# Weight splits of the latent-attention loop moved from VectorE to GpSimd

## The chip, the cores and the metric

One core of one Trainium2 chip. The metric is the device time of one execution in microseconds, median of several runs. Engines: PE is TensorE, DVE is VectorE, ACT is ScalarE, POOL is GpSimd, SP issues most of the DMAs.

## What is computed

Two blocks of two layers each on 512 tokens of width 1024, all in float32. The last layer is the one that matters here, a latent attention with 16 heads:

```python
q_lat = einsum('bshd,rhd->bshr', q_nope, w_uk)
s = (q_lat . kv_c + q_rope . k_rope) * ATTN_SCALE      # per head, 512 x 512
p = softmax(where(key_chunk <= q_chunk, s, -inf))
o = einsum('bshr,rhd->bshd', p . kv_c, w_uv)
out = (o * silu(z)) @ w_out                            # z = h @ w_in[:, 448:]
```

## The kernel before

Weights come in 294 units of 128 x 1024 floats, through a ring of four slots (`raw`, `wsp`, `RING` = 4). A product in float32 is made of three matmuls (`mm3`), so each unit is split in two parts, high and low. ACT copies the unit to float32r (`split_hi`, counted by `hi_done`). Then the low part, raw minus high, is made by POOL (`split_lo`, line 445) or, in the loop over pairs of heads, by DVE (`weights_lo`, line 2044); both count `w_ready`, on which PE and the next load wait. PE counts `unit_used` when it is done with a unit, and `split_hi` of the unit four places later waits for that.

The latent attention runs over eight pairs of heads, 0 to 7, in a loop of two pairs a turn (r = 0, 1); the last two pairs are written out behind the loop. A pair uses four units, from u0: `z` of the first head (u0), `z` of the second (u0 + 1), the query weights of the next pair (u0 + 2), and values of this pair with latent keys of the next (u0 + 3). In a pair the splits run ahead: ACT makes the high parts of u0 + 3 and u0 + 4 near the start of the softmax, and of u0 + 5 and u0 + 6 at the end of the pair.

Within a pair PE projects `z`, then goes through eight blocks m = 0 to 7 (two heads, four blocks of queries, 128 to 512 keys wide). For each block: scores (lines 1379 to 1382), on DVE the maximum (`o_max_of`, 2025 and 2027), on ACT the exponential (`o_exp_of`, 875), on DVE the reciprocal of the sum and the normalisation in place (`o_norm`, 2032 and 2034), on PE transposes (`o_transpose`, 1390), on ACT their copy (`o_turn`, 883), on PE the product with the latents (`o_latent`, 1398). Parts of the projection of the second `z` are put between blocks. Behind the blocks come the next pair's queries, the values, and the next pair's latent queries. DVE rotates the query's rope part (`rotate`, 2015 to 2020), ACT copies its high part (`rope_hi`, 860), and POOL makes the low part (`rope_lo`, 505), on 64 partitions, twice a pair; the scores of a head wait for it (`r_ready`).

Every engine takes its instructions in the order in which they are written; nothing is planned at run time. In the loop POOL has only `rope_lo` before the change. After the loop it waits until all of the loop's units are split (`w_ready` at O_O), and then splits the 16 units of the output projection. The first two of these fall in the softmax of pair 7.

Of the kernel before, what the change touches and what calls it, by code (L numbers as in the profile page):

```python
# [16 lines left out]
F32 = mybir.dt.float32  # L17
# [3 lines left out]
ALU = mybir.AluOpType  # L21
# [8 lines left out]
PAIRS = HEADS // 2  # L30
# [7 lines left out]
RING = 4  # L38
# [21 lines left out]
O_H = O_C + 4  # L60
O_O = O_H + 33
UNITS = O_O + 16
# [45 lines left out]
def build(nc, xT, weights, cols, rows, c_row, rel, onehot, w2, posc, ada, ws, bs, pcnt, pos, out):  # L108

    ctx = ExitStack()  # L110
    with ctx:
        def sb(name, shape, dt=F32):
            return ctx.enter_context(nc.sbuf_tensor(name, shape, dt))

        def sem(name):
            return ctx.enter_context(nc.semaphore(name))
# [4 lines left out]
        raw = sb("raw", [P, RING, UNIT])  # L121
        wsp = sb("wsp", [P, RING, 2, UNIT], F32R)
# [80 lines left out]
        last = mid[:, 16:22, :].rearrange("p a t -> p (a t)")  # L203
# [37 lines left out]
        hi_done, w_ready, unit_used = sem("hi_done"), sem("w_ready"), sem("unit_used")  # L241
# [178 lines left out]
        def _(pool):  # L420
# [22 lines left out]
            def split_lo(slot, unit):  # L443
                pool.wait_ge(hi_done, unit + 1)
                pool.tensor_tensor(wsp[:, slot, 1, :], raw[:, slot, :], wsp[:, slot, 0, :].bitcast(F32),  # L445
                                   ALU.subtract).then_inc(w_ready, 1)
# [54 lines left out]
            def rope_lo(hp):  # L501

                for e in range(2):
                    pool.wait_ge(r_hi, hp * 4 + (2 * e + 2))
                    pool.tensor_tensor(qrs[e][1][0:HD, :], r_raw[e], qrs[e][0][0:HD, :].bitcast(F32), ALU.subtract  # L505
                                       ).then_inc(r_ready, 1)
# [3 lines left out]
                if u == O_H + 4:  # L510
                    rope_lo(0)
            with pool.Fori(0, PAIRS - 1) as hp:
                rope_lo(hp + 1)
            pool.wait_ge(w_ready, O_O)
            for u in range(O_O, UNITS):
                split_lo(u % RING, u)


# [1 line left out]
        def _(act):  # L520
            def split_hi(u, i=0):

                if u >= UNITS:
                    return
                act.wait_ge(raw_in[u % RING], i * 16 + 16 * (u // RING + 1))
                if u >= RING:
                    act.wait_ge(unit_used, i * RING + (u + 1 - RING))
                act.activation(wsp[:, u % RING, 0, :], raw[:, u % RING, :], ACT.Copy).then_inc(hi_done, 1)  # L528
# [262 lines left out]
            for g in range(4):  # L791
                u0 = E_X + 5 * g
# [57 lines left out]
            def nope_hi(r, hp):  # L850
                for e in range(2):
                    act.wait_ge(uq_mm, hp * 3 + (3 * r + e + 1))
                    act.activation(qns[:, e, 0, :], bank[GATE_BANKS[r % 2][e]][:, :], ACT.Copy).then_inc(n_hi, 1)

            def rope_hi(r, hp):

                for e in range(2):
                    act.wait_ge(r_part, hp * 4 + (4 * r + e + 3))
                    for half in range(2):
                        act.activation(qrs[e][0][half * HD:half * HD + HD, :], r_raw[e], ACT.Copy).then_inc(r_hi, 1)  # L860

            def keep_latent(r, hp):

                act.wait_ge(lat_mm, hp + (r + 1))
                act.activation(ql[0], bank[4][:, :], ACT.Copy).then_inc(ql_ready, 1)
                act.wait_ge(unit_used, hp * RING + (O_H + 2 + RING * r))
                act.activation(ql[1], bank[5][:, :], ACT.Copy).then_inc(ql_ready, 1)

            def o_exp_of(m, r, hp):

                b, w = m % 2, P * (m % 4 + 1)
                if m >= 2:
                    act.wait_ge(o_t, hp * 8 + (8 * r + m - 1))
                act.wait_ge(o_nm, hp * 8 + (8 * r + m + 1))
                act.activation(o_p[b][:, 0:w], bank[SCORE_BANKS[r][b]][:, 0:w], ACT.Exp, scale=QK_SCALE,
                               bias=stat[:, b, 1:2], accum_out=stat[:, b, 2:3]).then_inc(o_exp, 1)

            def o_turn(m, r, hp):
                b, w = m % 2, P * (m % 4 + 1)
                if m >= 2:  # L880
                    act.wait_ge(o_pv, hp * 8 + (8 * r + m - 1))
                act.wait_ge(o_t, hp * 8 + (8 * r + m + 1))
                act.activation(o_pt[b][:, 0:w], bank[2 + b][:, 0:w], ACT.Copy).then_inc(o_pt_ready, 1)

            def latent_hi(e, r, hp):
                act.wait_ge(o_pv, hp * 8 + (8 * r + 4 * e + 4))
                act.activation(ols[:, e, 0, :], bank[4 + e][:, :], ACT.Copy).then_inc(ol_hi, 1)

            def pair_of_heads(r, hp, last):

                u0 = O_H + 2 + RING * r
                split_hi(u0 + 3, hp)
                for m in range(10):
                    if m >= 2:
                        o_turn(m - 2, r, hp)
                    if m < 8:
                        o_exp_of(m, r, hp)
                    if m == 0:
                        split_hi(u0 + 4, hp)
                    if m == 8:  # L900
                        latent_hi(0, r, hp)
                for e in range(2):
                    act.wait_ge(unit_used, hp * RING + (u0 + e + 1))
                    act.wait_ge(mid_ready, hp * 2 + (2 * r + MID_O - 1 + e))
                    act.activation(zs[e], bank[GATE_BANKS[r][e]][:, :], ACT.Silu).then_inc(z_ready, 1)
                latent_hi(1, r, hp)
                if last:
                    split_hi(u0 + 5, hp)
                else:
                    nope_hi(r + 1, hp)  # L910
                    split_hi(u0 + 5, hp)
                    split_hi(u0 + 6, hp)
                    keep_latent(r + 1, hp)
                    rope_hi(r + 1, hp)

            act.wait_ge(kr_ready, 2)
            act.wait_ge(consts, 12)
# [529 lines left out]
        def _(dve):  # L1447
# [461 lines left out]
            for g, window in enumerate(WINDOWS):  # L1909
                u0 = E_X + 5 * g  # L1910
# [118 lines left out]
            def o_norm(m, r, hp):  # L2029
                b, w = m % 2, P * (m % 4 + 1)  # L2030
                dve.wait_ge(o_exp, hp * 8 + (8 * r + m + 1))
                dve.reciprocal(stat[:, b, 3:4], stat[:, b, 2:3]).then_inc(o_rec, 1)
                dve.wait_ge(o_rec, hp * 8 + (8 * r + m + 1))
                dve.tensor_scalar(o_p[b][:, 0:w], o_p[b][:, 0:w], stat[:, b, 3:4], None, ALU.mult).then_inc(o_prob, 1)

            def latent_lo(e, r, hp):
                dve.wait_ge(ol_hi, hp * 2 + (2 * r + e + 1))
                dve.tensor_tensor(ols[:, e, 1, :], bank[4 + e][:, :], ols[:, e, 0, :].bitcast(F32), ALU.subtract
                                  ).then_inc(ol_ready, 1)

            def weights_lo(u, hp):

                dve.wait_ge(hi_done, hp * RING + (u + 1))
                dve.tensor_tensor(wsp[:, u % RING, 1, :], raw[:, u % RING, :], wsp[:, u % RING, 0, :].bitcast(F32),
                                  ALU.subtract).then_inc(w_ready, 1)

            def pair_of_heads(r, hp, last):

                u0 = O_H + 2 + RING * r
                for m in range(10):  # L2050
                    if 1 <= m < 9:
                        o_norm(m - 1, r, hp)
                    if m < 8:
                        o_max_of(m, r, hp)
                    if m in (3, 5) and not last:
                        weights_lo(u0 + m // 2 + 2, hp)
                    if m == 9:
                        latent_lo(0, r, hp)
                latent_lo(1, r, hp)
                if not last:  # L2060
                    nope_lo(r + 1, hp)
                    rotate(r + 1, hp)
                for e in range(2):
                    if last and e:
                        dve.wait_ge(unit_used, hp * RING + (u0 + 3))
                    else:
                        dve.wait_ge(uv_mm, hp * 2 + (2 * r + e + 1))
                    dve.wait_ge(z_ready, hp * 2 + (2 * r + e + 1))
                    dve.tensor_tensor(mid[:, hp * 2 + (2 * r + e), :], bank[GATE_BANKS[r][e]][:, :], zs[e], ALU.mult
                                      ).then_inc(mid_ready, 1)  # L2070
                if not last:
                    weights_lo(u0 + 5, hp)
                    weights_lo(u0 + 6, hp)

            nope_lo(0, 0)
            rotate(0, 0)
            residual(1)
            dve.wait_ge(w_ready, O_H + 5)
            with dve.Fori(0, PAIRS - 2, 2) as hp:
                for r in range(2):  # L2080
                    pair_of_heads(r, hp, False)
# [142 lines left out]
```

## Time and profile before

| | |
|---|---|
| median of 3 runs | 2074.91 us (2074.57 to 2076.23) |
| profiled execution | 2074.91 us, span 2073.2 us |
| PE busy | 1962.0 us, 95% |
| DVE busy | 1025.1 us, 49% |
| ACT busy | 841.7 us, 41% |
| POOL busy | 750.2 us, 36% |
| loop over pairs of heads | about 1689 to 1955 us |

Busy time is the time in which an engine has an instruction under way. A timeline row gives the start in microseconds from the span's start, the duration in microseconds, the engine, the line of the kernel, the operation, out<-in, the shape, and how many instructions are merged in the row; in brackets how long the engine was idle before and who ended that. Matmuls are pipelined, so they overlap in the records.

### The profile page before, as it was taken

What the parts mean: (1) busy time and instruction counts of PE and PEld (TensorE: products, weight loads), DVE (VectorE), ACT (ScalarE), POOL (GpSimd) and SP (SyncE); (2) the same over time, 40 slices, a digit from 0 to 9 for tenths busy, and PEclk for the clock granted to TensorE, in tenths of its full rate; (3) what the DMA queues carried; (4) which work ended last, traced back from release to release, by engine and by line L of the source; (5) the groups of instructions that cost most, each with busy time, mean ns of one, the idle gap of its engine ahead of it and who ended that gap; (6) DMA issues with size and microseconds to landing.
All of it is one profiled execution on the core that took longest, in us unless ns stands there. A gap on an engine that the chain in (4) does not pass through costs nothing.

```text
span 2073.2 us, 29104 instructions
## 1 busy us (share of the span) xinstructions
PE 1962.0 (95%) x9640; PEld 1633.5 (79%) x9640; DVE 1025.1 (49%) x2314; ACT 841.7 (41%) x1520; POOL 750.2 (36%) x354
## 2 busy tenths in 40 slices
PE   7999999999988999999999997999999789999896
PEld 5897888888777888878888886877888568787784
DVE  5554655221536766546563214666411576666514
ACT  4564222222443766543222324322222356565533
POOL 4533544444363100136444442545544121010340
PEclk9999999999998988999999999999999999999999
DMA  7532554222242112026543322322222121111121
GB/s 252 153 105 97 187 177 165 95 100 99 84 142 77 47 46 63 25 81 203 176 168 101 102 91 82 102 92 97 92 101 91 51 71 61 61 61 61 62 81 40
DMA packets 70026, 209.55 MB, mean 101 GB/s; under 512 B 9739, under 2 KB 15115, under 8 KB 69948
## 3 DMA queue, kind: packets, MB, share of 16 engines
q1 hardware_dynamic: 57724, 174.72, 25.2%
q10 hardware_dynamic: 12224, 33.85, 5.0%
q8 instruction: 41, 0.67, 0.1%
q14 instruction: 37, 0.30, 0.0%
HBM read 196.90 MB, written 8.49 MB: 99 GB/s over the span
## 4 chain that ended last, share of the span: by engine, by line
PE 61%; issue 21%; POOL 9%; DVE 7%; ACT 2%; POOLq 0%; DVEq 0%; ACTq 0%
PE bank L946 15%; PE bank L948 15%; PE bank L947 15%; POOL wsp L445 9%; PE bank L1224 3%; PE bank L1398 1%; PE bank L1197 1%; PE bank L1379 1%; PE bank L1208 1%; PE bank L1092 1%; PE bank L1390 1%; PE bank L1069 1%; PE bank L1220 1%; PE bank L980 1%; PE bank L1080 1%
## 5 line engine op out<-in xcount | busy, mean ns | idle before, releaser
L445 POOL TENSOR_TENSOR wsp<-raw,wsp 128x1024 fp32r<-128x1024 f32 x266 | 664.8, 2505 | 884.5 <-ACT wsp L528 884.5
L946 PE MATMUL bank<-xs,wsp 128*128 128x512 f32 x1320 | 522.1, 396 | 19.2 <-issue 8.4
L948 PE MATMUL bank<-xs,wsp 128*128 128x512 f32 x1320 | 516.3, 391 | 0.0
L947 PE MATMUL bank<-xs,wsp 128*128 128x512 f32 x1320 | 516.2, 391 | 0.0
L528 ACT ACTIVATE wsp<-raw 128x1024 fp32r<-128x1024 f32 x294 | 307.5, 1053 | 237.3 <-PE bank L948 211.1
L946 PEld LDWEIGHTS bank<-xs,wsp 128*128 128x128 f32 x1320 | 249.8, 189 | 76.7 <-issue 15.2
L946 PE MATMUL bank<-xk,wsp 128*128 128x512 f32 x752 | 294.8, 392 | 9.4 <-DVE xk L1500 5.1
L948 PE MATMUL bank<-xk,wsp 128*128 128x512 f32 x752 | 294.0, 391 | 0.0
L947 PE MATMUL bank<-xk,wsp 128*128 128x512 f32 x752 | 294.0, 391 | 0.0
L948 PEld LDWEIGHTS bank<-xs,wsp 128*128 128x128 f32 x1320 | 249.3, 189 | 52.7
L947 PEld LDWEIGHTS bank<-xs,wsp 128*128 128x128 f32 x1320 | 249.6, 189 | 52.1 <-issue 1.4
L1500 DVE TENSOR_TENSOR xk<-mid,xk 128x512 fp32r<-128x512 f32 x86 | 61.1, 711 | 381.2 <-ACT xk L568 381.2
L568 ACT ACTIVATE xk<-mid 128x512 fp32r (+1 forms) x86 | 54.3, 631 | 328.1 <-PE bank L948 328.1
L946 PEld LDWEIGHTS bank<-xk,wsp 128*128 128x128 f32 x752 | 142.0, 189 | 41.4 <-DVE xk L1500 6.3
L948 PEld LDWEIGHTS bank<-xk,wsp 128*128 128x128 f32 x752 | 142.1, 189 | 29.5
L947 PEld LDWEIGHTS bank<-xk,wsp 128*128 128x128 f32 x752 | 142.2, 189 | 29.4
L1550 DVE CUSTOM_DVE_ANT_0 gen<-gen 128x1024 f32<-128x1024 f32 x48 | 125.8, 2621 | 12.9 <-issue 12.9
L584 ACT ACTIVATE tmp<-tmp 128x512 f32<-128x512 f32 x44 | 27.8, 632 | 245.4 <-DVE tmp L1538 245.4
L505 POOL TENSOR_TENSOR mid_r<-tmp,mid_r 64x512 fp32r<-64x512 f32 x16 | 30.9, 1945 | 217.4 <-ACT mid_r L860 217.3
L1540 DVE TENSOR_TENSOR mid<-bank,rstd 128x512 f32 (+1 forms) x44 | 30.4, 692 | 155.3 <-PE bank L948 155.3
L1224 PE MATMUL bank<-mid 128*128 128x64 f32 x640 | 90.0, 292 | 0.0
L731 ACT ACTIVATE mid<-mid,stat 128x128 f32<-128x128 f32 (+3 forms) x128 | 70.8, 554 | 39.0 <-DVE stat L1802 38.5
(287 smaller groups left out, 2554.3 us busy)
## 6 DMA issues: line engine op xcount, KB each, us to landing
raw<-weights SPq DMA_DIRECT2D x294, 512.0 KB, 3.4
gen<-ada ACTq DMA_DIRECT2D x48, 512.0 KB, 3.6
tmp<-mid SPq DMA_DIRECT2D x64, 128.0 KB, 2.8
bias_b<-bias_row ACTq DMA_DIRECT2D x1, 4096.0 KB, 37.0
mid<-bias_b SPq DMA_DIRECT2D x8, 512.0 KB, 3.9
hT<-xT SPq DMA_DIRECT2D x2, 1024.0 KB, 9.3
bias_a<-bias_row ACTq DMA_DIRECT2D x1, 2048.0 KB, 16.2
mid<-bias_a SPq DMA_DIRECT2D x8, 256.0 KB, 2.8
```

Source lines behind the costliest of these rows:

```text
L445: pool.tensor_tensor(wsp[:, slot, 1, :], raw[:, slot, :], wsp[:, slot, 0, :].bitcast(F32), ALU.subtract).then_inc(w_ready, 1)
L505: pool.tensor_tensor(qrs[e][1][0:HD, :], r_raw[e], qrs[e][0][0:HD, :].bitcast(F32), ALU.subtract).then_inc(r_ready, 1)
L528: act.activation(wsp[:, u % RING, 0, :], raw[:, u % RING, :], ACT.Copy).then_inc(hi_done, 1)
L568: act.activation(xk[:, k % 2, 0, :], mid[:, i * RING + k, :], ACT.Copy).then_inc(xk_hi, 1)
L731: act.activation(b_s[b][:, r, 0:w], b_s[b][:, r, 0:w], ACT.Exp, scale=-1.0, bias=stat[:, b, r:r + 1], accum_out=stat[:, b, 4 + r:5 + r]).t ...
L946: pe.matmul(dst, w[0], x[0], start=first, stop=False)
L947: pe.matmul(dst, w[0], x[1], start=False, stop=False)
L948: return pe.matmul(dst, w[1], x[0], start=False, stop=last)
L1224: x = pe.matmul(dst[:, (1 + r) * HD:(2 + r) * HD], b_pt[b][:, r, kb * P:kb * P + P], vtok[:, r, kb * P + pp * HD:kb * P + pp * HD + HD], s ...
L1500: dve.tensor_tensor(xk[:, k % 2, 1, :], mid[:, i * RING + k, :], xk[:, k % 2, 0, :].bitcast(F32), ALU.subtract).then_inc(xk_ready, 1)
L1540: dve.tensor_tensor(mid[:, i * 2 + p, :], bank[2 * p + 1][:, :], rstd[:, :], ALU.mult).then_inc(up_free, 1)
L1550: dve.tensor_tensor_reduce(out=ada_st[k], in0=ada_st[k], in1=cond, scale=1.0, scalar=0.0, op0=ALU.mult, op1=ALU.add, accum_out=mod_sum[:, ...
```

## The change

The low parts of all units of the loop are made by POOL; `weights_lo` and its four calls a pair leave DVE's order. In POOL's loop, written over seven pairs, three splits come ahead of `rope_lo` and one behind it. On ACT the high part of unit u0 + 6 moves behind `keep_latent` and `rope_hi`. The two waits for `w_ready` that handed the splits from POOL to DVE and back are gone.

```diff
@@ POOL
             with pool.Fori(0, PAIRS - 1) as hp:
-                rope_lo(hp + 1)
-            pool.wait_ge(w_ready, O_O)
-            for u in range(O_O, UNITS):
+                for k in range(RING):
+                    u = O_H + 5 + k
+                    split_lo(u % RING, hp * RING + u)
+                    if k == 2:
+                        rope_lo(hp + 1)
+            for u in range(O_H + 5 + RING * (PAIRS - 1), UNITS):
                 split_lo(u % RING, u)
@@ ACT, pair_of_heads
                     nope_hi(r + 1, hp)
                     split_hi(u0 + 5, hp)
-                    split_hi(u0 + 6, hp)
                     keep_latent(r + 1, hp)
                     rope_hi(r + 1, hp)
+                    split_hi(u0 + 6, hp)
@@ DVE
-            def weights_lo(u, hp):
-
-                dve.wait_ge(hi_done, hp * RING + (u + 1))
-                dve.tensor_tensor(wsp[:, u % RING, 1, :], raw[:, u % RING, :], wsp[:, u % RING, 0, :].bitcast(F32),
-                                  ALU.subtract).then_inc(w_ready, 1)
...
-                    if m in (3, 5) and not last:
-                        weights_lo(u0 + m // 2 + 2, hp)
...
-                if not last:
-                    weights_lo(u0 + 5, hp)
-                    weights_lo(u0 + 6, hp)
...
-            dve.wait_ge(w_ready, O_H + 5)
```

## Rows read from the trace of the kernel before

**Rows 1.** The page, busy time of each engine and its share of the span
```profile
PE 1962.0 (95%) x9640; PEld 1633.5 (79%) x9640; DVE 1025.1 (49%) x2314; ACT 841.7 (41%) x1520; POOL 750.2 (36%) x354
```
**Rows 2.** Busy time by stretch, one pair: stretch, length, engines, granted clock, DMA
```profile
1795.70:1829.70 34.00, 33.48 (x177) 27.38 (x176) 21.30 (x48) 21.24 (x43) 3.99 (x2) 1.00 0.19 63
```
**Rows 3.** Instructions by line: count, duration min/median/max in ns, first and last start
```profile
L445 POOL TENSOR_TENSOR wsp<-raw,wsp x266: 2346/2399/3686, 10.0 to 2026.7; 128x1024 fp32r<-128x1024 f32 x133
...
L2044 DVE TENSOR_TENSOR wsp<-raw,wsp x28: 1214/1226/2320, 1699.6 to 1927.1; 128x1024 fp32r<-128x1024 f32 x28
...
L505 POOL TENSOR_TENSOR mid_r<-tmp,mid_r x16: 1283/1766/2276, 1684.9 to 1928.3; 64x512 fp32r<-64x512 f32 x16
```
**Rows 4.** Timeline of DVE in pair 3
```profile
1795.47 0.29 DVE L2034 TENSOR_SCALAR gen<-gen,stat 128x128 f32<-128x128 f32 x1
...
1801.69 1.23 DVE L2044 TENSOR_TENSOR wsp<-raw,wsp 128x1024 fp32r<-128x1024 f32 x1
```
**Rows 5.** Timelines of ACT, POOL, DVE and PE in pair 7
```profile
1927.82 1.06 ACT L528 ACTIVATE wsp<-raw 128x1024 fp32r<-128x1024 f32 x1
...
1926.56 3.98 POOL L505 TENSOR_TENSOR mid_r<-tmp,mid_r 64x512 fp32r<-64x512 f32 x2 [30.29 <-ACT mid_r L860]
...
1930.51 2.38 POOL L445 TENSOR_TENSOR wsp<-raw,wsp 128x1024 fp32r<-128x1024 f32 x1
...
1932.86 2.36 POOL L445 TENSOR_TENSOR wsp<-raw,wsp 128x1024 fp32r<-128x1024 f32 x1
...
1931.75 3.55 DVE L2034 TENSOR_SCALAR gen<-gen,stat 128x128 f32<-128x128 f32 x1
...
1935.36 0.33 PE L1390 MATMUL bank<-ident,gen 128*128 128x128 f32 x1 [1.38 <-DVE gen L2034]
...
1937.06 0.44 PE L1390 MATMUL bank<-ident,gen 128*128 128x128 f32 x2 [0.38 <-DVE gen L2034]
...
1950.45 2.07 PE L1398 MATMUL bank<-gen 128*128 128x128 f32 x14
```
**Rows 6.** Timeline of PE in pair 3
```profile
1797.31 0.40 PE L948 MATMUL bank<-xs,wsp 128*128 128x512 f32 x1
...
1798.65 0.38 PE L1390 MATMUL bank<-ident,gen 128*128 128x128 f32 x2
...
1812.14 2.07 PE L1398 MATMUL bank<-gen 128*128 128x128 f32 x14
```
**Rows 7.** Timeline of POOL around the start of pair 4
```profile
1824.27 3.99 POOL L505 TENSOR_TENSOR mid_r<-tmp,mid_r 64x512 fp32r<-64x512 f32 x2 [30.01 <-ACT mid_r L860]
```
**Rows 8.** Timeline of ACT, pair 3 and the start of pair 4
```profile
1794.78 0.37 ACT L875 ACTIVATE gen<-bank,stat 128x128 f32<-128x128 f32 x1 [0.88 <-DVE stat L2027]
...
1795.14 1.05 ACT L528 ACTIVATE wsp<-raw 128x1024 fp32r<-128x1024 f32 x1
...
1817.48 1.05 ACT L528 ACTIVATE wsp<-raw 128x1024 fp32r<-128x1024 f32 x1
...
1822.92 2.59 ACT L860 ACTIVATE mid_r<-tmp 64x512 fp32r<-64x512 f32 x4
```
**Rows 9.** Timelines of DVE and POOL in earlier layers
```profile
41.68 1.68 DVE L1612 TENSOR_SCALAR mid<-mid,bq  x1
...
43.03 2.58 POOL L445 TENSOR_TENSOR wsp<-raw,wsp 128x1024 fp32r<-128x1024 f32 x1
...
1455.31 0.71 DVE L1961 TENSOR_SCALAR gen<-gen 128x512 f32<-128x512 f32 x1
```
**Rows 10.** Timeline of ACT at the start of pair 0
```profile
1694.49 1.04 ACT L528 ACTIVATE wsp<-raw 128x1024 fp32r<-128x1024 f32 x1
```
**Rows 11.** PE's timeline after two stops, and the stretch behind the second, granted clock 0.50
```profile
788.42 0.69 PE L1220 MATMUL bank<-gen 128*128 128x64 f32 x2 [2.41 <-DVE gen L1829]
...
1955.02 0.73 PE L946 MATMUL bank<-xk,wsp 128*128 128x512 f32 x1 [2.50 <-DVE xk L2038]
...
1955.05:1958.47 3.42, 2.83 (x6) 1.74 (x6) 1.24 (x2) 0.64 (x3) 2.37 (x1) 0.50 0.02 5
```

## The prediction

> **What bounds the kernel now.** I read the page's totals first, then busy time by pair of heads, then each engine's timeline through one pair, and last the timeline of pair 7, the only one in which GpSimd (POOL) splits weights next to the softmax. TensorE (PE) is busy 1962.0 of 2073.2 us [rows 1]. The change touches the loop over the eight pairs of heads (0 to 7), about 265 us. There a pair takes 34.00 us and PE is busy 33.48 of them [rows 2]. So whatever VectorE (DVE) gives back can bring at most 0.5 us a pair, 4 us in all: 0.2%. The reader should see this cap first: in this loop the kernel has no PE time to win.
>
> The profiled execution took 2074.91 us with a span of 2073.2, and 2074.91 is also the median of the three runs. I add to that.
>
> **The change, part by part.**
>
> *Removed from DVE:* four weight splits a pair, 1.23 us each when undisturbed, 28 in all [rows 3]. One stands behind the maximum of block 3 (1801.69 in pair 3) [rows 4], one behind that of block 5, two at the end of a pair. The last two run while PE does the next gate's projection; after them DVE waits for scores. The two inside the softmax delay a normalisation, but PE has pieces of a projection to fill in. Pair 7 has no such splits and is the measure: from transpose(1) to PE's last group it takes 1950.45 - 1937.06 = 13.39 us [rows 5], pair 3 takes 1812.14 - 1798.65 = 13.49 [rows 6]. The gain is 0.1 us a pair, and it is in the working below, which uses pair 7's rhythm.
>
> *Added to POOL:* 28 splits at 2.40 us [rows 3]. POOL is idle 30.01 us of each 34 [rows 7], so its total is no issue. When does each run? Call the units of a pair a, b (gate projections), c (queries of the next pair) and d (values). Around the start of pair 4:
> - b is copied by ScalarE (ACT) from 1817.48 to 1818.53 [rows 8], so POOL splits it by 1820.95. PE wants it behind the first scores of pair 4, near 1828.8. Hidden.
> - rope_lo needs ACT's rotated halves, 1822.92 to 1825.51 [rows 8]. Its second operation starts at 1825.55 and takes 1.28 us undisturbed [rows 3], now that no DVE split runs beside it: done 1826.83.
> - c: ACT's copy moves behind rope_hi, 1825.53 to 1826.58. That takes 1.06 us ahead of exp(0), of which 0.88 was idle [rows 8]: exp(0) comes 0.2 us late, which PE, with a projection piece to do, does not see. POOL splits c from 1826.85 to 1829.23.
> - d, and a of the next pair: both copied by 1830.4 (1795.14 + 1.05 + 34.00 + 0.2 for the later one), so POOL goes on without a pause, 1829.2 to 1831.6 and 1831.6 to 1834.0.
>
> So a run of three POOL operations now lies from 1826.85 to 1834.0, on top of the softmax's first steps.
>
> **What that run meets.** norm(0), the normalisation of block 0, is a DVE tensor_scalar that reads and writes SBUF. In pair 3 it took 0.29 us [rows 4]. In pair 7, with two POOL splits beside it, the same instruction took 3.55 us, from 1931.75 to 1935.30, when POOL's run was over, and PE stood still 1.38 us ahead of transpose(0) [rows 5].
>
> The Trainium skill (SBUF — State Buffer, "Who interferes with whom") says that DVE in a two-port mode and GpSimd share one pair of ports, held for a whole instruction, with the other fully blocked. That there is a block, the trace agrees; by that rule DVE would wait for one instruction here, not two, and the sum would be the first rival's.
>
> Which is it? In 17 places DVE asks during a POOL operation that a split follows directly. In 16 of them DVE goes in between: the first is the bias multiply at 41.68, which ends at 43.36, 0.3 us behind the start of POOL's second (2.58 us, lengthened for it), the last is at 1455.31 [rows 9]. Only norm(0) of pair 7 waits for both, and there the second split is not lengthened (2.36). What is special: ahead of both stands rope_lo, on 64 partitions, which ended at 1930.54, while the split behind it had been released by 1928.88 [rows 5]. My reading, an inference from one case: the half of GpSimd that has no part in a 64-partition operation begins the next one early, and from then on some part of it is always busy. The new run has this order too: c is released at 1826.58, rope_lo ends at 1826.83. I take pair 7's case, as it is the same instruction with the same neighbours, and the other as the first rival.
>
> The Trainium skill (GPSIMD Engine Reference, "2.1 Instruction dispatch") says that each core starts the next instruction as soon as it has done its own share. No row here shows single cores.
>
> **The sum.**
> 1. Pairs 1 to 6: norm(0) asks at 1795.47 + 34.00 + 0.2 = 1829.67 [rows 4], in d's split, and ends at 1834.05. From its end to PE's last group pair 7 takes 1950.45 - 1935.30 = 15.15 us [rows 5]. So the last group starts at 1849.20, against 1812.14 + 34.00 = 1846.14 [rows 6]: +3.06 us, six times: 18.4.
> 2. Pair 0 has no c split between rope_lo and the softmax, and rope_lo is long done. I take the usual order: norm(0) slips in between d and a, norm(1) waits for a. a's copy runs 1694.49 to 1695.53 and d's right before it [rows 10]; POOL 1694.25 to 1699.05. transpose(1) comes at 1699.25, plus 13.39 is 1712.6, against 1812.14 - 3 x 34.00 = 1710.1: +2.5.
> 3. Pair 7 had two splits; now c is in front of them and the run ends 1.0 later: +1.0.
> 4. Clock. PE stands still from 1831.7 (its last filler starts at 1797.31 + 34.00 and runs 0.40 [rows 6]) to 1834.1: 2.4 us. Stops of 2.41 and 2.50 us in this trace were each followed by half the granted clock, 1.2 GHz; behind the second it lasted 3.42 us, with six matmuls in 2.83 us [rows 11]. Pair 7's stop of 1.38 us was not. 3.4 us at half clock cost 1.7 us of matmul time; part of it lies where PE waits anyway, so I take 1.2, in six of the eight pairs, as the stops are at the short end: 7.2.
>
> Sum: 18.4 + 2.5 + 1.0 + 7.2 = 29.1, so 2074.9 + 29.1 = 2104 us, 1.4% slower. Bounds of this case: no drop of the clock, 2097; a drop in every pair at its full 1.7 us, 2110, and 2112 with 0.2 us a pair more of waits behind it.
>
> **Rivals.**
> - *DVE goes in between two POOL operations*, as in 16 of 17 places. norm(0) ends at 1831.7, norm(1) asks at 1833.2 and waits for a's split; transpose(1) comes at 1834.2, plus 13.39 is 1847.6: +1.45 for pairs 1 to 6 (8.7), +2.5 for pair 0; pair 7 gains 0.7, as its norm(0) no longer waits for two. 2074.9 + 10.5 = 2085.4. PE's stops are then about 1.3 us, shorter than pair 7's, so no clock term.
> - *No net loss.* PE's filler hides the waits: 0 to 4 us, 2075 to 2079. Against it: norm(0) asks 2.8 us behind the run's start and 4.3 ahead of its end, and in pair 7 the filler did not hide a shorter wait.
> - *Faster.* DVE meets nothing of POOL, and the idle 0.5 us a pair goes: 2074.9 - 8 x 0.5 = 2071. It needs POOL's run to be over by 1829.67, so three splits in 2.8 us, under 0.95 us each instead of 2.40.
> - *Units late for PE.* b is ready 7.8 us early, c and d more; no row speaks for it.
>
> **How the numbers follow.** Block through the run with drops of the clock 0.55, without 0.10; DVE in between 0.23; no net loss 0.07; faster 0.02; dearer than 2112 0.03. The low end, 2084, takes in the first rival and leaves out the cheap ones. 0.2% (4 us) is about what a measurement can tell from no change, so the 2071 of the third rival lies mostly within it: faster 0.01, within 0.08, slower 0.91.
>
> **What would show it.** In the new trace: four L445 splits a pair, b alone ahead of rope_lo and three without a pause behind it; norm(0) at about 4.4 us in pairs 1 to 6, reductions and one-column operations unchanged; PE idle about 2.4 us ahead of transpose(0), released by it; stretches of half clock behind most; pairs 37 to 38 us apart. If norm(0) takes about 2 us and norm(1) about 1 instead, the first rival holds. I am wrong altogether if a pair stays at 34.0.

## The result and the profile after

The changed kernel takes 2105.3 us (median of 4, 2102.7 to 2109.1) against 2074.7: ratio 1.0149, 95% interval 1.0132 to 1.0167. The forecast was 2104.

The profiled execution has a span of 2103.0 us, 29.8 more than before. POOL's and DVE's timelines around the start of pair 4, and DVE's at the start of pair 0, where the run is two splits and no rope_lo stands right ahead:

```profile
1833.42 2.40 POOL L445 TENSOR_TENSOR wsp<-raw,wsp 128x1024 fp32r<-128x1024 f32 x1 [22.38 <-ACT wsp L531]
1839.09 2.60 POOL L505 TENSOR_TENSOR mid_r<-tmp,mid_r 64x512 fp32r<-64x512 f32 x2 [3.27 <-ACT mid_r L863]
1841.65 7.02 POOL L445 TENSOR_TENSOR wsp<-raw,wsp 128x1024 fp32r<-128x1024 f32 x3
...
1844.00 2.39 POOL L445 TENSOR_TENSOR wsp<-raw,wsp 128x1024 fp32r<-128x1024 f32 x1
...
1843.40 0.15 DVE L2030 TENSOR_SCALAR stat<-stat 128x1 f32<-128x1 f32 x1
...
1844.36 4.41 DVE L2037 TENSOR_SCALAR gen<-gen,stat 128x128 f32<-128x128 f32 x1
1848.69 0.41 DVE L2028 TENSOR_REDUCE stat<-bank 128x1 f32<-128x256 f32 x1
...
1850.12 0.35 DVE L2037 TENSOR_SCALAR gen<-gen,stat 128x256 f32<-128x256 f32 x1
...
1695.16 1.93 DVE L2037 TENSOR_SCALAR gen<-gen,stat 128x128 f32<-128x128 f32 x1
...
1698.44 1.02 DVE L2037 TENSOR_SCALAR gen<-gen,stat 128x256 f32<-128x256 f32 x1
```

The reader is to see the row with x3: c, d and a without a pause from 1841.65 to 1848.67, and norm(0) ending 0.10 us behind it. The row with x1 below it is d alone. norm(0) asked 2.71 us into the run, 0.36 us behind the start of d, and did not get in at the one border still ahead of it, that between d and a. In pair 0 it waited for one split only (1.93 us), and norm(1) for the other (1.02). That is the same instruction, with the same splits, once blocked through a run and once let in.

PE's timeline at the same two places, and busy time in the stretch behind the stop of pair 4 and the one after it (the column ahead of the last two is the granted clock):

```profile
1848.82 0.33 PE L1393 MATMUL bank<-ident,gen 128*128 128x128 f32 x1 [2.32 <-DVE gen L2037]
...
1849.35 1.09 PE L1384 MATMUL bank<-gen_r,mid_r 128*128 128x384 f32 x1
...
1697.14 0.47 PE L1393 MATMUL bank<-ident,gen 128*128 128x128 f32 x1 [5.74 <-DVE gen L2037]
...
1849.33:1852.74 3.41, 3.41 (x9) 1.81 (x8) 1.65 (x6) 1.67 (x6) 0.00 (x0) 0.50 0.47 169
1852.74:1856.15 3.41, 3.41 (x24) 3.01 (x23) 1.96 (x7) 1.16 (x3) 0.00 (x0) 1.00 0.00 0
```

The clock is 1.2 GHz in the first 3.41 us and 2.4 GHz in the next. "PE busy" is 3.41 in both and does not tell them apart, and the counts (9 and 24 matmuls) do not measure it either, as the matmuls of the first stretch are wider. The same matmul does: this L1384 takes 1.09 us here and 0.63 us at full clock in e2_filler. Every pair from 1 to 7 has one such stretch, pair 0 a double one. The chain of waits around pair 4 has the stall as its largest piece:

```profile
1841.43 1.28 ACT L531
1842.72 0.91 ACT wsp L531
...
1844.36 4.42 DVE gen L2037
1848.82 0.33 PE bank L1393
```

The reader also sees ACT's table load and its copy of d on the chain ahead of it, as exp(0) comes behind them. The run on POOL starts when rope_lo ends, at 1841.69, and that waited for ACT's rope_hi. c had been copied by 1841.41, so in this trace ACT's copy of c does not set when DVE is shut out.

Where the 29.8 us are, read off PE's timelines (a pair is from its first scores, counted from their first matmul of line 1384, before the change 1381, to those of the next; pair 7 to its last transpose):

| | before | after | more |
|---|---|---|---|
| up to pair 1's first scores | 1725.7 | 1729.5 | 3.8 |
| pairs 1 to 6 | 204.4 | 225.9 | 21.5 |
| pair 7 | 20.5 | 22.2 | 1.6 |
| the rest | 122.6 | 125.5 | 2.9 |

The rest holds the same instructions in both. Busy time over it, before and then after:

```profile
1950.60:2073.20 122.60, 100.52 (x423) 78.44 (x421) 36.63 (x52) 39.53 (x54) 33.46 (x14) 0.95 0.17 60
...
1977.50:2103.00 125.50, 103.48 (x423) 79.92 (x421) 36.66 (x52) 39.60 (x54) 33.43 (x14) 0.93 0.17 59
```

The mean granted clock is 0.95 before and 0.93 after. In the traces of the experiments this part's length goes with that number: 121.5 us at 0.96 (e2_filler, e8_tail), 125.0 and 125.1 at 0.92 (e3_behind, e1_settle).

### The profile page after: what moved, and what is told of

It reads as the page before. It is cut to its first block, busy times and chain, and to the rows that moved or that the text cites. A ratio compares the mean times of both kernels' runs of the same rounds, so it can differ in the third digit from the quotient of the medians.

```text
span 2103.0 us, 29110 instructions
## 1 busy us (share of the span) xinstructions
PE 1975.6 (94%) x9640; PEld 1638.0 (78%) x9640; DVE 1016.6 (48%) x2286; ACT 840.0 (40%) x1520; POOL 805.9 (38%) x382
## 4 chain that ended last, share of the span: by engine, by line
PE 58%; issue 21%; POOL 9%; DVE 8%; ACT 4%; POOLq 0%; DVEq 0%; ACTq 0%
PE bank L949 14%; PE bank L951 14%; PE bank L950 14%; POOL wsp L445 9%; PE bank L1227 3%; PE bank L1382 2%; DVE gen L2037 2%; PE bank L1200 1%; PE bank L1401 1%; PE bank L1211 1%; PE bank L1095 1%; PE bank L1393 1%; ACT wsp L531 1%; PE bank L1072 1%; PE bank L1223 1%
## 5 line engine op out<-in xcount | busy, mean ns | idle before, releaser
L445 POOL TENSOR_TENSOR wsp<-raw,wsp 128x1024 fp32r<-128x1024 f32 x294 | 730.5, 2491 | 1051.4 <-ACT wsp L531 1051.3
L951 PEld LDWEIGHTS bank<-xk,wsp 128*128 128x128 f32 x752 | 142.2, 189 | 29.8
L1227 PEld LDWEIGHTS bank<-mid 128*128 128x128 f32 x640 | 84.7, 209 | 0.0
```

Source lines behind the costliest of these rows:

```text
L951: return pe.matmul(dst, w[1], x[0], start=False, stop=last)
L1227: x = pe.matmul(dst[:, (1 + r) * HD:(2 + r) * HD], b_pt[b][:, r, kb * P:kb * P + P], vtok[:, r, kb * P + pp * HD:kb * P + pp * HD + HD], s ...
```

## The experiments

A table first; times in us, "pair" is the mean of pairs 1 to 6, norm(0) and norm(1) those of pair 3 or 4. Each ratio is to runs of the kernel before taken alongside; their medians were 2074.2 to 2074.9.

| | median | ratio to before, 95% | pair | norm(0) | norm(1) | half clock in pairs 1 to 7 |
|---|---|---|---|---|---|---|
| before | 2074.9 | | 34.06 | 0.29 | 0.35 | none |
| the change | 2105.3 | 1.0132 to 1.0167 | 37.65 | 4.41 | 0.35 | each |
| e1_settle | 2088.1 | 1.0044 to 1.0075 | 35.37 | 2.32 | 1.02 | none |
| e2_filler | 2097.7 | 1.0098 to 1.0129 | 36.85 | 4.48 | 0.35 | none |
| e3_behind | 2073.9 | 0.9984 to 1.0002 | 34.04 | 0.29 | 0.35 | none |
| e4_no_split | 2074.9 | 0.9989 to 1.0007 | 34.04 | 0.29 | 0.35 | none |
| e5_half | 2105.3 | 1.0136 to 1.0177 | 38.19 | 4.87 | 0.35 | nearly each |
| e6_whole | 2077.0 | 1.0003 to 1.0022 | 34.06 | 0.29 | 1.05 | none |
| e7_two_two | 2074.3 | 0.9991 to 1.0008 | 34.12 | 0.29 | 0.36 | none |
| e8_tail | 2074.8 | 0.9991 to 1.0008 | 34.05 | 0.29 | 0.35 | none |
| e9_c_ahead | 2079.8 | 1.0013 to 1.0032 | 34.41 | 0.70 | 1.26 | none |

**e1_settle**

```diff
                     if k == 2:
                         rope_lo(hp + 1)
+                        pool.wait_ge(r_ready, hp * 2 + 4)
```

> The changed kernel, but POOL waits for its own two rope_lo operations to be finished (r_ready) before it takes the split of unit c. Nothing else moves; c starts at the same time to within 0.1 us. Theory (a 64-partition operation lets half of GpSimd run ahead, and DVE then never finds a moment between two splits): with all parts of GpSimd level again, DVE goes in between d and a. norm(0) takes about 2 us instead of 4.4, norm(1) about 1 us instead of 0.35, PE's stop ahead of transpose(0) shrinks from 2.3 us to almost nothing and one of about 1.3 us comes ahead of transpose(1), no half clock in pairs 1 to 7; pairs about 35.5 us, 2085 us in all. Rival (DVE loses to any run of three splits, or this instruction always loses): norm(0) stays at 4.4 us, pairs at 37.6, 2105 us.

Timelines of POOL, DVE and PE in pair 4:

```profile
1834.65 7.06 POOL L445 TENSOR_TENSOR wsp<-raw,wsp 128x1024 fp32r<-128x1024 f32 x3 [0.16 <-POOL mid_r L505]
...
1837.00 2.40 POOL L445 TENSOR_TENSOR wsp<-raw,wsp 128x1024 fp32r<-128x1024 f32 x1
...
1837.17 2.32 DVE L2038 TENSOR_SCALAR gen<-gen,stat 128x128 f32<-128x128 f32 x1
...
1840.85 1.02 DVE L2038 TENSOR_SCALAR gen<-gen,stat 128x256 f32<-128x256 f32 x1
...
1839.55 0.33 PE L1394 MATMUL bank<-ident,gen 128*128 128x128 f32 x1 [0.24 <-DVE gen L2038]
...
1841.92 0.33 PE L1394 MATMUL bank<-ident,gen 128*128 128x128 f32 x1 [1.05 <-DVE gen L2038]
```

There is a pause of 0.16 us behind rope_lo. The run of three behind it is as long as in the changed kernel and 2.5 us old when norm(0) asks, again in d. Now DVE gets in at the border between d and a: norm(0) ends at 1839.49 and d at 1839.40. 17 us come back. 2088.1 is 3 above the forecast; pairs 1 to 6 give 7.9 of the 13 lost (8.7 in the rival's sum).

**e5_half and e6_whole**

```diff
                     split_lo(u % RING, hp * RING + u)
+                    if k == 3:
+                        pool.tensor_tensor(stdb[0:64, 0:64], stdb[0:64, 64:128], stdb[0:64, 128:192], ALU.subtract)
                     if k == 2:
                         rope_lo(hp + 1)
+                        pool.wait_ge(r_ready, hp * 2 + 4)
```

In e6_whole `0:64` ahead of the comma is `0:128` in all three operands.

> The kernel of e1 (POOL waits for its rope_lo before c), with one small POOL operation added between the splits c and d: 64 partitions x 64 columns of a scratch tile, about 0.3 us; nothing is left out. d has been released long before c ends. Theory (a 64-partition operation in a queue that goes on at once lets half of GpSimd start the next one early, and after it no moment is free for DVE): the block through the whole run is back although the wait of e1 is still there: norm(0) about 4.7 us instead of 2.3, norm(1) 0.35, stops of about 2.6 us ahead of transpose(0) with half clock behind them, pairs 37.7 to 38.0, 2107 us. Rival (what e1 healed was the pause that its wait made behind rope_lo): norm(0) 2.6 us, pairs 35.6, 2090 us.

> The same as e5_half but the small operation has 128 partitions x 64 columns. It is the control: same place, same columns. Theory: no part of GpSimd gets ahead, so DVE goes in between d and a as in e1: norm(0) 2.3 to 2.6 us, norm(1) 1.0, no half clock in pairs 1 to 7, pairs 35.6, 2090 us. Rival (any third or fourth operation in the run shuts DVE out, whatever its partitions): as e5_half, pairs 37.9, 2107 us.

Timelines of POOL and DVE, first of e5_half:

```profile
1802.33 2.38 POOL L445 TENSOR_TENSOR wsp<-raw,wsp 128x1024 fp32r<-128x1024 f32 x1 [0.16 <-POOL mid_r L505]
1804.67 0.32 POOL L517 TENSOR_TENSOR stdb<-stdb 64x64 f32<-64x64 f32 x1
1804.95 4.68 POOL L445 TENSOR_TENSOR wsp<-raw,wsp 128x1024 fp32r<-128x1024 f32 x2
...
1804.84 4.87 DVE L2040 TENSOR_SCALAR gen<-gen,stat 128x128 f32<-128x128 f32 x1
```

then of e6_whole:

```profile
1797.06 2.38 POOL L445 TENSOR_TENSOR wsp<-raw,wsp 128x1024 fp32r<-128x1024 f32 x1 [0.16 <-POOL mid_r L505]
1799.40 0.32 POOL L517 TENSOR_TENSOR stdb<-stdb 128x64 f32<-128x64 f32 x1
1799.68 4.81 POOL L445 TENSOR_TENSOR wsp<-raw,wsp 128x1024 fp32r<-128x1024 f32 x2
...
1799.57 0.29 DVE L2040 TENSOR_SCALAR gen<-gen,stat 128x128 f32<-128x128 f32 x1
...
1801.21 1.05 DVE L2040 TENSOR_SCALAR gen<-gen,stat 128x256 f32<-128x256 f32 x1
```

This is the pair that decides. Both have e1's wait, and a small operation of 0.32 us in which norm(0) asks, 0.17 us behind its start. With 128 partitions DVE goes in by its end, ahead of d, and at the next border (norm(1)) again; POOL's two splits take 4.81 us for it. With 64 partitions DVE waits 4.87 us, past two borders, for d and a as well, and these take 4.68. 28 us hang on the number of partitions of one small instruction. e6_whole is 13 us better than forecast: I had not seen that norm(0) would ask inside the small operation, which is over at once, and not in d. In its trace norm(1) takes 1.05 us in pairs 1 to 7 and a pair is still 34.06 us; what remains of the loss is in pair 0, which is as long as in the changed kernel (42.0 us).

**e2_filler**

```diff
                 project(u0 + 1, z[1][:, :], hp, part=range(4))
+                for _ in range(10):
+                    pe.matmul(bank[2][:, :], tile(u0 + 1, 0)[0], xin(0)[0], start=True, stop=True)
```

> The changed kernel with ten more matmuls a pair (128 x 512, result thrown away, into the bank that transpose(0) overwrites) where PE stands still ahead of transpose(0); work is added, none is left out. Theory (the half clock behind each stop of 2.3 us costs about 1.2 us a pair on its own): ten matmuls at 0.23 us fill the stop, norm(0) still takes 4.4 us, the granted clock stays at 1.00 through pairs 1 to 7, pairs 36.2 to 36.5 us instead of 37.6, 2095 to 2098 us. Rival (the clock costs nothing, as PE waits for DVE and ACT in these 3.4 us anyway): 2105 us or, as matmuls were added, more.

Timelines of PE and DVE in pair 4, and busy time over a pair:

```profile
1841.05 2.43 PE L1415 MATMUL bank<-xs,wsp 128*128 128x512 f32 x10
1843.60 0.33 PE L1393 MATMUL bank<-ident,gen 128*128 128x128 f32 x1
...
1844.12 0.63 PE L1384 MATMUL bank<-gen_r,mid_r 128*128 128x384 f32 x1
...
1839.07 4.48 DVE L2039 TENSOR_SCALAR gen<-gen,stat 128x128 f32<-128x128 f32 x1
...
1800.10:1836.90 36.80, 36.07 (x187) 29.09 (x187) 19.96 (x42) 21.01 (x43) 12.01 (x7) 1.00 0.17 57
```

DVE waits as long as in the changed kernel, but the clock stays at 1.00 and the pair is 0.80 us shorter (36.85 against 37.65), with more work in it. So 0.80 us of the 3.59 a pair are the clock's, 2.8 the stall's own. The 7.6 us in the medians are 5.6 for seven pairs and 2 within the scatter of these runs.

**e3_behind**

```diff
             with pool.Fori(0, PAIRS - 1) as hp:
+                pool.wait_ge(o_prob, hp * 8 + 8)
                 for k in range(RING):
...
+            pool.wait_ge(o_prob, 8 * PAIRS)
             for u in range(O_H + 5 + RING * (PAIRS - 1), UNITS):
```

> All splits on POOL as in the changed kernel, but POOL waits for the last normalisation of a pair (o_prob) before it takes d and a, so that they lie between the softmaxes of two pairs: d and a about 2.4 us each from the end of norm(7), then b, rope_lo, c. c ends at about 0.4 us ahead of norm(0). Theory (all of the loss is the block of norm(0), with its clock): norm(0) 0.29 us again, pairs 33.9 to 34.0, and pair 7, whose two splits move too, 2 us shorter than before: 2071 to 2073 us, so 2 to 4 us faster than before. Rival (POOL's splits hurt elsewhere, or d and a come late for PE): pairs above 34.3, 2077 us or more.

Timelines of POOL and DVE:

```profile
1814.51 4.72 POOL L445 TENSOR_TENSOR wsp<-raw,wsp 128x1024 fp32r<-128x1024 f32 x2 [16.55 <-DVE gen L2039]
1821.39 2.40 POOL L445 TENSOR_TENSOR wsp<-raw,wsp 128x1024 fp32r<-128x1024 f32 x1 [2.15 <-ACT wsp L533]
1827.05 2.60 POOL L505 TENSOR_TENSOR mid_r<-tmp,mid_r 64x512 fp32r<-64x512 f32 x2 [3.26 <-ACT mid_r L865]
1829.61 2.37 POOL L445 TENSOR_TENSOR wsp<-raw,wsp 128x1024 fp32r<-128x1024 f32 x1
...
1832.31 0.29 DVE L2039 TENSOR_SCALAR gen<-gen,stat 128x128 f32<-128x128 f32 x1
```

All 28 splits are on POOL, and the kernel is back at 2073.9. d and a now lie between the softmaxes, beside DVE operations that read PSUM (`bank`) and are not longer for it (0.69 us); c ends at 1831.98, 0.33 ahead of norm(0). The whole loss was where the splits lay. The 2 to 4 us of gain that I expected are not there: 2073.9 is 0.9 above the range and the interval includes 1, though pair 7 is 1.8 us shorter in the trace.

**e4_no_split**

```diff
-                    split_lo(u % RING, hp * RING + u)
+                    at = slice(0, 8)
+                    pool.wait_ge(hi_done, hp * RING + u + 1)
+                    pool.tensor_tensor(wsp[:, u % RING, 1, at], raw[:, u % RING, at],
+                                       wsp[:, u % RING, 0, at].bitcast(F32), ALU.subtract).then_inc(w_ready, 1)
```

> The changed kernel with POOL's 28 splits of the loop cut to 8 of their 1024 columns; the low parts of these weights are mostly left out, so the output is not the reference's. It shows the order of the changed kernel without POOL's load. Theory (taking the splits off DVE gives 0.1 us a pair, all else was POOL's time on DVE's way): norm(0) 0.29 us, pairs 33.9, pair 7 as before, so 2073 to 2075 us. Rival (the moved ACT copy or the order itself costs): above 2077 us.

Busy time over one pair:

```profile
1800.00:1834.00 34.00, 33.38 (x176) 27.38 (x176) 15.88 (x43) 21.11 (x42) 3.35 (x6) 1.00 0.20 62
```

DVE has 15.88 us of work in place of 21.30 [rows 2], POOL has next to nothing, ACT's copy of c is behind rope_hi, and the pair is 34.0, not the 33.9 expected. Relieving DVE of its splits is worth nothing here, even free of charge.

**e7_two_two** (against the kernel before: DVE keeps d and a, POOL takes b and c; ACT's copy of c is moved as in the change)

```diff
-                rope_lo(hp + 1)
-            pool.wait_ge(w_ready, O_O)
+                pool.wait_ge(w_ready, hp * RING + (O_H + 7))
+                split_lo((O_H + 7) % RING, hp * RING + (O_H + 7))
+                rope_lo(hp + 1)
+                split_lo((O_H + 8) % RING, hp * RING + (O_H + 8))
+            pool.wait_ge(o_prob, 8 * PAIRS)
...
                 dve.wait_ge(hi_done, hp * RING + (u + 1))
+                dve.wait_ge(w_ready, hp * RING + u)
...
-                if not last:
-                    weights_lo(u0 + 5, hp)
-                    weights_lo(u0 + 6, hp)
```

> The work shared: DVE keeps d and a at their places inside the softmax, POOL takes b (ahead of rope_lo) and c (behind it), with waits on w_ready to keep the order of the units; the two splits of the output projection that fall in pair 7 wait for that pair's last normalisation. Nothing is left out. Theory (the loss comes only from POOL splits that run when norm(0) or norm(1) asks; c ends 0.4 us ahead of norm(0)): norm(0) 0.29 us, pairs 34.0, pair 7 shorter by 1.8 us: 2072 to 2074 us. Rival (c runs into norm(0), or the two engines wait for each other): norm(0) 0.6 us or more, pairs 34.3 or more, 2077 us.

The mechanism went as expected (norm(0) 0.29, pair 7 18.7 us in place of 20.5), and the median, 2074.3, is 0.3 above the range; the saved 1.8 us are within the scatter.

**e8_tail** (against the kernel before)

```diff
             pool.wait_ge(w_ready, O_O)
+            pool.wait_ge(o_prob, 8 * PAIRS)
```

> The kernel before, with one wait more: POOL starts the splits of the output projection only behind the last normalisation of pair 7 (o_prob). Nothing is left out. It measures by itself what two POOL splits in the softmax cost. Theory: norm(0) of pair 7 takes 0.29 us instead of 3.55, and from pair 7's first scores to its last transpose it takes 18.7 us instead of 20.5; all pairs before stay at 34.0: 2072.5 to 2073.5 us, 1.8 us faster than before. Rival (the two splits are then late for the output projection and give it back): 2074.9 us.

DVE's timeline in pair 7:

```profile
1929.08 0.29 DVE L2035 TENSOR_SCALAR gen<-gen,stat 128x128 f32<-128x128 f32 x1
```

0.29 us where before had 3.55 [rows 5], and 18.73 us from first scores to last transpose in place of 20.52. That is the 1.8 us forecast, in the trace. The medians, 2074.8 against 2074.5, do not show it, and 2074.8 is above the range: executions of one kernel scatter by several us, so this stays unsettled as a gain in time.

**e9_c_ahead**

```diff
                     split_hi(u0 + 5, hp)
+                    split_hi(u0 + 6, hp)
                     keep_latent(r + 1, hp)
                     rope_hi(r + 1, hp)
-                    split_hi(u0 + 6, hp)
...
-                    if k == 2:
+                    if k == 3:
                         rope_lo(hp + 1)
```

> The changed kernel with the order of before kept for unit c: ACT copies it ahead of keep_latent and rope_hi, POOL splits it ahead of rope_lo. Then the run at the softmax is d and a alone, and d is released by ACT only after rope_lo has ended. Theory: c (POOL, about 2.4 us) now meets DVE's two additions of rotate, the first of which takes about 3 us instead of 0.7, so rope_hi and exp(0) come 0.5 to 1.5 us late; norm(0) goes in between d and a (under 2.4 us), norm(1) waits for a. Pairs 35 to 36 us, 2082 to 2090 us, no half clock. Rival (the order of c is what counts and two splits do no harm to the softmax): 34.0 and 2075; or d and a block norm(0) as a run as in pair 7 of before: norm(0) 3.5 to 4.5 us, pairs 37 and 2100 us.

Timelines of POOL, ACT and DVE in pair 3:

```profile
1797.09 2.60 POOL L505 TENSOR_TENSOR mid_r<-tmp,mid_r 64x512 fp32r<-64x512 f32 x2 [1.95 <-ACT mid_r L863]
1799.64 2.39 POOL L445 TENSOR_TENSOR wsp<-raw,wsp 128x1024 fp32r<-128x1024 f32 x1
1802.21 2.38 POOL L445 TENSOR_TENSOR wsp<-raw,wsp 128x1024 fp32r<-128x1024 f32 x1 [0.17 <-ACT wsp L531]
...
1798.35 1.06 ACT L531 ACTIVATE wsp<-raw 128x1024 fp32r<-128x1024 f32 x1
...
1792.80 3.61 DVE L2023 TENSOR_TENSOR tmp<-tmp 64x512 f32<-64x512 f32 x2
...
1801.41 0.70 DVE L2037 TENSOR_SCALAR gen<-gen,stat 128x128 f32<-128x128 f32 x1
...
1803.47 1.26 DVE L2037 TENSOR_SCALAR gen<-gen,stat 128x256 f32<-128x256 f32 x1
```

c on POOL lengthens the two additions of rotate (3.61 us for both, 1.40 without it), but this does not lengthen the pair: pairs 1, 3 and 5 are 34.05 to 34.07 us, where I had expected 35 to 36. I was also wrong on d in these pairs: ACT has copied it by 1799.41, rope_lo ends at 1799.69, and d follows without a pause, as in the blocked cases. But a is not copied before 1802.13, so the queue pauses for 0.17 us behind d, and there norm(0) gets in. So such a pause ends the block even with rope_lo right ahead of the split. In pairs 2 and 4 (34.98 us) d starts 1.09 us behind rope_lo, d and a are a run without a pause, and norm(0) goes in at their border (1.99 us). The time, 2079.8, is 2 under the range.

## Why the prediction was right

*The cap* held: e4_no_split gives 34.04 us a pair. The 0.1 us a pair that I read out of pair 7's rhythm was not there.

*The run and when norm(0) asks* held: three splits without a pause, of 7.02 us (forecast 7.15), norm(0) 4.41 (4.4), PE's stop 2.32 (2.4), rope_lo 1.29 each, reductions and one-column operations unchanged.

*Blocked through, or in between*, was the open step, put at 0.65 against 0.23. Blocked through is what happened. I took one case against sixteen because it had the same neighbours, and named the 64-partition operation ahead as the reason. Pair 0 of the changed kernel, without it, behaves as the sixteen. A wait behind it (e1_settle) restores the usual order; a 64-partition operation of 0.3 us put back into the queue brings the block again, a 128-partition one does not (e5_half, e6_whole). That the number of partitions of an operation ahead in the unbroken queue decides is shown, for 64 with 128 behind it; other counts were not tried. 64 partitions alone do not do it: in before, DVE's split asked during the first of two rope_lo operations in each of pairs 1 to 7, and went in at the border between them (2.32 us at 1824.80, where 1.23 is usual). That half of GpSimd gets ahead and so some part always works is the reading that forecast the block, its end in e1_settle and its return in e5_half, but single cores are in no trace.

The Trainium skill (GPSIMD Engine Reference, "2.1 Instruction dispatch") has this as each core's starting the next instruction when its own share is done; e5_half and e6_whole agree, 4.87 us against 0.29. The Trainium skill's rule of the shared ports (SBUF — State Buffer, "Who interferes with whom"), by which the loser waits for the whole of one instruction, gives e1_settle's 2.32 us and pair 0's 1.93, and not the changed kernel's 4.41.

*The terms.* Pairs 1 to 6: 18.4 for the stall and their share of the clock, 5.4, so 23.8 forecast and 21.5 measured. The stall took 2.79 us a pair against 3.06, and the clock term was sized too high per drop (1.2 us against 0.80) and too rare (six pairs against all eight).

Pair 0: 2.5, or 3.4 with an even share of the clock, against 3.8 up to pair 1. From the pair's first exponential to pair 1's first scores, which leaves out the scatter ahead of it, it is 31.6 us before and 35.0 after, so 3.4. norm(0) and norm(1) went as forecast. PE's stop there grew from 1.60 to 5.74 us, and only 1.64 of that is norm(0)'s. The other 2.5 come from the clock ahead of the pair:

```profile
1678.60:1685.40 6.80, 5.26 (x13) 4.13 (x14) 6.67 (x10) 4.62 (x8) 2.85 (x2) 0.50 0.31 107
...
1678.60:1685.40 6.80, 4.94 (x22) 4.11 (x23) 6.67 (x9) 5.35 (x10) 3.19 (x2) 1.00 0.32 119
```

The first row is before, at half clock; the second is after, at full clock. After, PE is through its filler 2.5 us earlier and then stands longer, while norm(0) comes when DVE and ACT let it. e4_no_split shows that part by itself, with next to nothing on POOL: a stop of 4.10 us. e1_settle, at half clock ahead of the pair like before, has a stop of 3.25, 1.64 of it norm(0)'s. What I had not seen is the double stretch of half clock behind the stop, in every kernel with POOL's splits there (the changed one, e1, e2, e5, e6, e9) and in none without; e4_no_split has a single one.

Pair 7: 1.0, or 1.9 with its share of the clock, against 1.6. The rest of the kernel took 2.9 more, which was in no term; it goes with the granted clock, as the rows under the table of the 29.8 us show. That the sum came out at 29.1 against 29.8 is in part luck: the terms were too large for the loop by more than 2 us, and no run shows that the 2.9 come from the change.

## What to carry to other kernels

Moving work from a busy engine to an idle one is judged by what runs beside it at each moment, not by totals: here the same 28 splits on POOL cost 30 us at one place and nothing at another (e3_behind), and freeing DVE was worth nothing, since PE was the bound. Look in the trace of before for one place where the two already overlap: pair 7 had the price in it. If VectorE must get in between 128-partition GpSimd operations, keep 64-partition ones out of the unbroken queue ahead of them, or wait for them.

## What the runs showed of the hardware that was not expected

A GpSimd operation on 64 partitions changed what came behind it for as long as the queue was unbroken: 0.32 us of work made VectorE wait 4.87 us instead of 0.29, and pauses of 0.16 and 0.17 us (e1_settle, e9_c_ahead) ended it. There was a second loss: a stop of TensorE of 2.31 us a pair cost another 0.80 us through the granted clock, which ten thrown-away matmuls gave back, so that more work took less time (2097.7 against 2105.3 us).

The clock did not follow from the stop alone. The stop of 2.50 us behind the loop is in every trace; in eight of them half clock came with it, in e2_filler, e6_whole and e8_tail it did not, and one stop of 2.80 us in e5_half (pair 4) brought none. The scatter between executions of one kernel goes with it too: those of the kernel before ran from 2072.2 us, at a mean granted clock of 0.980, to 2080.4, at 0.974.
